# Key and query norms at the end of the projection's program, with another order of work in the sampled and mixing stages

## The chip, the cores and the metric

The kernel runs on one core of one Trainium2 chip. The metric is the device time of one execution in microseconds; three runs of a kernel are compared by their median.

## What is computed

One step of a one-layer hybrid decoder over 1104 tokens: 1040 of a prompt (16 meta tokens ahead) and 64 sampled ones, eight sequences of eight. Cut to what the change touches:

```
proj = rmsnorm(x) @ w_in                       # 1024 -> 5136 columns, split into three head groups
q, k = l2norm(silu(conv(q))) * 128**-0.5, l2norm(silu(conv(k)))
beta = sigmoid(b); g = -exp(a_log) * softplus(a + bias); G = cumsum(g) in a chunk
# gated DeltaNet, per chunk and head: A = I + tril(beta k k') exp(G_i - G_j); solve with [beta v, beta k exp(G)]
o = (q exp(G)) S + tril(q k' dec) w;   S = exp(G_last) S + (k exp(G_last - G))' w
# Mamba-2 SSD, per chunk: y = tril(C B' dec) xdt + (C exp(G)) h;  h = exp(G_last) h + B' xdt
# short convolution of 512 channels; then
x = x + concat(gated norms of the three) @ w_out;  x = x + moe(rmsnorm(x));  y = rmsnorm(x)
```

The prompt goes through in chunks from a zero state. The sampled tokens start from given states, so that each of their eight sequences has its own 128x128 state per head.

## The kernel before

Activations are held transposed, channels on partitions and tokens along the free axis. All products of the projections are made of three products of split operands (`copy_hi` on ScalarE takes a rounded high part, `take_lo` on VectorE the rest). The stages are separate programs, one `Block` each with one instruction list per engine, and a stage starts when every engine has ended the one before. Inside a stage the order is written out by hand; semaphores named in `REC_PE`, `SAM_DVE` and the like count steps, and SP and POOL issue the DMAs in the order written, waiting in line.

**Projection** (`projection_phase`). 40 blocks of 128 columns, two PSUM halves. VectorE scales, convolves and splits weights, ScalarE applies silu. The last 12 blocks are the short convolution; VectorE's last step there (L604 to L614) ends in a store by POOL (L435), a second one for the kept rows (L476), and SP waits for both (L336). `Gates` makes the gate rows early in the stage: `rows_a`, `rows_b`, `rows_c` hold four or twelve rows each at partitions 0, 32, 64, 96.

**Recurrence** (`recurrence_phase`). Before the first chunk it squares keys and queries (L904), sums them over the channels with a picking matrix on TensorE (L1114), takes logarithms on ScalarE (L907, L910) and puts them into the rows on VectorE (L995 to L1004), so that the l2 norms are folded into the decay exponents. SP stores three of the row groups to `g_dram` (L801 to L803) and, when these have landed, loads rows of it broadcast over the partitions, for each chunk: `rc_gb` (L783, L778), `rc_eb` (L791), `rc_egs` (L793). Ahead of that SP loads `x`, `bcs`, `d_skip` and the first `rc_gb` half (L796 to L798, L778). TensorE turns the rows into columns (L1123). POOL makes the decay tables (L826 to L843) and decayed states (L852, L854); then ten chunks of 104 tokens follow, one chain through the engines each.

**Sampled tokens** (`sampled_phase`). SP loads the rows table `ds_gb`, the two states `ds_s` and `ds_ss` and `d_skip`, in this order. ScalarE's exponential of the table comes first, VectorE multiplies it onto the keys, TensorE multiplies the 64 small pieces of the keys with the eight states (L1501), then the triangular products, then the queries with the states (L1501), the SSD pieces (L1546), and the state updates (L1560, L1571) with operands spread over the sequences by VectorE. `S1` and `spread` have two buffers for four heads.

**Output projection** (`mix_phase`). Nine tiles of 128 tokens. `w_out` comes in eight chunks of 768 KB through two landing buffers (`chunk`), each split by ScalarE and VectorE. VectorE's `gate` makes the gated rows; `scale` normalises them; TensorE's `out(t, h)` makes half h of tile t, 36 products. `gate` waits for four constants:

```
dve.wait_ge(consts, 64)
dve.scalar_tensor_tensor(mix[:, 0:4, 0:n], q[:, :, cols(t)], ow[:, 0:1], z[:, 0:4, 0:n], ...)
```

After it `expert_phase` sorts the tokens by expert and runs 33 blocks of experts; it isn't touched.

Of the kernel before, what the change touches and what calls it, by code (L numbers as in the profile page):

```python
# [17 lines left out]
ALU = mybir.AluOpType  # L18
# [3 lines left out]
P = 128  # L22
# [236 lines left out]
def projection_phase(nc, io, hn, gates, q, kv, ones, masks, xbc_dram, z_dram, yc_dram):  # L259
# [6 lines left out]
    with ExitStack() as stack:  # L266
# [6 lines left out]
        w1, rb = m.sb("c_w1", [P, KD]), m.sb("c_rb", [P, T])  # L273
        qkv, x, sq, ss_of = (q, kv[:, 0:HA], kv[:, HA:2 * HA]), kv, out, 1
# [7 lines left out]

        def pair(name):
            return [m.sem(f"c_{name}{h}") for h in range(2)]
# [4 lines left out]
        x_hi, x_lo = m.sem("c_xhi"), m.sem("c_xlo")  # L289
# [22 lines left out]
        with nc.Block() as block:  # L312
# [26 lines left out]
            def _(pe):  # L339
# [25 lines left out]
                with pe.Fori(1, NB_ALL // 2) as i:  # L365
                    for h in range(2):
                        pe.wait_ge(lo_done[h], i + 1)
                        pe.wait_ge(ps_free[h], i + 1)
                        block_(i, h)

            @block.scalar
            def _(act):
# [49 lines left out]
                for b in range(3 * NC - 2):  # L422
                    split_hi(act, *divmod(FIRST_C + b, 2))

# [54 lines left out]
            def _(dve):  # L479
# [66 lines left out]
                dve.wait_ge(gates.dve_step, 16)  # L546
                convolve(3, 1)
# [19 lines left out]
                for b in range(3 * NC):  # L567
# [10 lines left out]
                    if b < 3 * NC - 2:  # L578
                        split_lo(dve, i, h)
                    if b % 3 == 1:  # L580
# [17 lines left out]
                    if b % 3 == 2:  # L598
# [15 lines left out]
                        dve.tensor_tensor(o, o, rb[:], ALU.mult).then_inc(yc_done, 1)  # L614

# [55 lines left out]
def recurrence_phase(nc, io, qkv, x, bcs, rows, columns, g_dram, masks, xbc_dram):  # L671
# [16 lines left out]
    with ExitStack() as stack:  # L688
# [8 lines left out]
        dve_set, squared, summed, logs, rows_done, rows_sent = (m.sem("rc_set"), m.sem("rc_sq"), m.sem("rc_sum"),  # L697
                                                                m.sem("rc_log"), m.sem("rc_rows"), m.sem("rc_sent"))
# [6 lines left out]
        NQK, CB = 2 * HA, 4  # L705
        sq, pick, eps = sb("sq", [P, 2, T]), sb("pick", [P, NQK, 36]), sb("eps", [64, 1])
        spare = sb("spare", [64, 3])
        lnk, lnq = sq[:, 0], sq[:, 1]
# [20 lines left out]
        sums = ps[:, 5:8, 0:TW]  # L729
# [9 lines left out]

        def by_tile(ap):  # L740
            return ap.rearrange("p (n t) -> p n t", n=NT)
# [31 lines left out]
        def _(sp):  # L773
# [29 lines left out]
            sp.dma_start(g_dram[R_Q:R_K], lnq[ROW_G:ROW_G + HA, :]).then_inc(rows_sent, 16)  # L803
# [13 lines left out]
        def _(pool):  # L817
# [27 lines left out]
            pool.wait_ge(dve_set, 14)  # L845
# [13 lines left out]
            pool.wait_ge(dve_set, 5)  # L859
# [7 lines left out]
        def _(act):  # L867
# [33 lines left out]
            for b in range(NQK):  # L901
                if b >= 2:
                    act.wait_ge(summed, b - 1)
                act.activation(sq[:, b % 2, :], (keys, queries)[b // HA][:, b % HA, :], ACT.Square).then_inc(squared, 1)  # L904
            act.wait_ge(dve_set, 14)
            act.wait_ge(summed, NQK)
            act.activation(by_tile(lnq[ROW_G:ROW_G + HA, :]), sums[ROW_G:ROW_G + HA], ACT.Ln,  # L907
                           bias=eps[ROW_G:ROW_G + HA]).then_inc(logs, 1)
            act.wait_ge(rows_done, 1)
            act.activation(lnk[ROW_G:ROW_G + HA, :], lnk[0:HA, :], ACT.Ln).then_inc(logs, 1)  # L910
# [54 lines left out]
        def _(dve):  # L965
# [5 lines left out]
            dve.memset(pick[:], 0.0).then_inc(dve_set, 1)  # L971
            dve.memset(eps[:], DK * EPS).then_inc(dve_set, 1)
            dve.wait_ge(dve_set, 1)
            for b in range(NQK):
                at = b if b < HA else ROW_G + b - HA
                ins = dve.memset(pick[:, b, at:at + 1], 1.0 if b < HA else float(DK))
            ins.then_inc(dve_set, 1)
# [6 lines left out]
            dve.wait_ge(dve_set, 9)  # L984
            dve.tensor_tensor(neg16_t[:], neg16[:], neg_t, ALU.add).then_inc(dve_set, 1)
            dve.tensor_tensor(neg_off[:], neg_off[:], neg, ALU.add).then_inc(dve_set, 1)
            dve.wait_ge(dve_set, 11)
            dve.tensor_tensor(neg16[:], neg16[:], neg, ALU.add).then_inc(dve_set, 1)
            dve.scalar_tensor_tensor(neg16_t[:], ident, NEG, neg16_t[:], ALU.mult, ALU.add).then_inc(dve_set, 1)
            dve.wait_ge(dve_set, 13)  # L990
            dve.sem_inc(dve_set, 1)

# [1587 lines left out]
```

## Time and profile before

| what | value |
|---|---|
| median of 3 runs | 1576.05 us (1573.89 to 1579.41) |
| profiled execution | 1573.76 us, its span 1572.1 us |
| busy: TensorE | 1396.8 us (89%) |
| busy: VectorE, ScalarE, POOL | 947.4 (60%), 624.2 (40%), 308.8 (20%) |
| mean granted TensorE clock | 0.918 of full |
| recurrence starts | 541.94 |
| sampled stage starts | 830.85 |
| output projection starts | 936.56 |

Times are microseconds from the first instruction. A busy share is a mean over stages with different limits; what an edit is worth has to be read in its own stage. PE is TensorE's products, PEld its weight loads, DVE VectorE, ACT ScalarE, POOL GpSimd, SPq the queue of SyncE that issues most DMAs.

### The profile page before, as it was taken

Reading aid. Unit: us, or ns where it says so; the run is one execution under the profiler, and the core shown is the slowest. Engines: PE = TensorE matmul, PEld = TensorE weight load, DVE = VectorE, ACT = ScalarE, POOL = GpSimd, SP = SyncE. Lnnn points to the kernel's source line nnn. Section 1 sums busy time; section 2 is a strip of 40 time slices with the busy share of each in tenths; the row PEclk is TensorE's granted clock in tenths of the full one; section 3 lists DMA queues with packets and bytes.
Section 4 is the critical chain, followed back from the end, with each engine's and each line's share of the span. In section 5 each row is a group of like instructions: output and inputs, shape, how many; then the busy total and the mean of one; then the engine's idle time right before and its main releaser. Section 6 shows DMA issues by size and latency. Waiting matters only on the chain. (4 is left out here: it accounts for less than half of the span.)

```text
span 1572.1 us, 22657 instructions
## 1 busy us (share of the span) xinstructions
PE 1396.8 (89%) x8385; PEld 1246.3 (79%) x8385; DVE 947.4 (60%) x1307; ACT 624.2 (40%) x917; POOL 308.8 (20%) x328
## 2 busy tenths in 40 slices
PE   7899999999999769999997944999984999999990
PEld 5899999999999549998996813888863788888870
DVE  4579666421334227777662446555428899999973
ACT  5231212121001154454541004332322888888874
POOL 0011111100000026546430000100001333333321
PEclk9999999999999879999995556999985999999995
DMA  5011122223111253543513036523315699899948
GB/s 203 27 41 40 40 82 83 105 83 105 60 54 42 81 128 66 100 97 70 111 34 141 1 155 194 169 81 119 95 50 205 215 278 276 266 277 275 269 78 270
DMA packets 113207, 199.12 MB, mean 127 GB/s; under 512 B 63292, under 2 KB 84028, under 8 KB 108004
## 3 DMA queue, kind: packets, MB, share of 16 engines
q1 hardware_dynamic: 97556, 140.70, 28.6%
q0 software_dynamic: 15568, 57.37, 13.3%
q8 instruction: 46, 0.75, 0.2%
q14 instruction: 37, 0.30, 0.1%
HBM read 202.12 MB, written 49.41 MB: 160 GB/s over the span
## 5 line engine op out<-in xcount | busy, mean ns | idle before, releaser
L98 PE MATMUL c_ps<-hn_lo,c_whi 128*128 128x368 f32 x936 | 177.9, 332 | 5.6 <-DVEq L182 5.6
L98 PE MATMUL c_ps<-hn_hi,c_wlo 128*128 128x368 f32 x936 | 177.5, 332 | 0.0
L98 PE MATMUL c_ps<-hn_hi,c_whi 128*128 128x368 f32 x936 | 176.6, 331 | 0.0
L98 PEld LDWEIGHTS c_ps<-hn_lo,c_whi 128*128 128x128 f32 x936 | 160.8, 189 | 5.8 <-issue 5.8
L2233 DVE TENSOR_TENSOR e_winlo<-e_win,e_winhi 128x2048 fp32r<-128x2048 f32 x66 | 151.2, 2292 | 20.9 <-ACT e_winhi L2161 18.8
L98 PEld LDWEIGHTS c_ps<-hn_hi,c_wlo 128*128 128x128 f32 x936 | 160.8, 189 | 0.0
L98 PEld LDWEIGHTS c_ps<-hn_hi,c_whi 128*128 128x128 f32 x936 | 159.8, 188 | 0.0
L82 ACT CAST c_whi<-c_w 128x1024 fp32r<-128x1024 f32 x40 | 42.1, 1052 | 227.5 <-PE c_ps L98 227.5
L2161 ACT CAST e_winhi<-e_win 128x2048 fp32r (+1 forms) x66 | 122.7, 1914 | 5.5 <-DMA e_win<-in_w_gate_up 4.6
L2074 POOL DMA_INDIRECT x_rows<-e_ys,idx_out x33 | 81.8, 2478 | 146.7 <-ACT e_ys L2186 146.7
L526 DVE SCALAR_TENSOR_TENSOR c_y<-c_raw,c_taps,c_y 128x1128 f32<-128x1128 f32 x60 | 83.6, 1394 | 6.1 <-DVE c_y L522 0.2
L2408 DVE TENSOR_TENSOR e_wdnlo<-e_wdn,e_wdnhi 128x2048 fp32r<-128x2048 f32 x33 | 75.5, 2289 | 4.0 <-ACT e_wdnhi L2171 3.5
L87 DVE TENSOR_TENSOR c_wlo<-c_w,c_whi 128x1024 fp32r<-128x1024 f32 x40 | 48.7, 1217 | 47.4 <-ACT c_whi L82 47.4
L2171 ACT CAST e_wdnhi<-e_wdn 128x2048 fp32r (+1 forms) x33 | 63.2, 1916 | 32.6 <-PE e_psd L2125 21.4
L485 DVE TENSOR_TENSOR c_raw<-c_ps,c_rb 128x368 f32<-128x368 f32 (+1 forms) x80 | 30.0, 437 | 64.4 <-PE c_ps L98 63.7
L2101 PE MATMUL e_psg<-e_winhi,e_hthi 128*128 128x512 f32 x264 | 66.4, 394 | 0.0
L2101 PE MATMUL e_psg<-e_winlo,e_hthi 128*128 128x512 f32 x264 | 65.3, 390 | 0.0
L2101 PE MATMUL e_psg<-e_winhi,e_htlo 128*128 128x512 f32 x264 | 65.3, 389 | 0.0
L871 ACT COPY rc_m<-rc_ps 104x208 f32<-104x208 f32 x120 | 39.7, 332 | 64.2 <-PE rc_ps L1099 63.8
L1677 POOL DMA_DIRECT2D x_rows<-o_land x9 | 4.9, 540 | 303.7 <-ACT o_land L1725 303.7
L1873 PE MATMUL o_psx<-o_whi,o_mixhi 128*128 128x512 f32 (+1 forms) x216 | 57.7, 419 | 3.8 <-ACT o_mixhi L82 3.8
L2101 PEld LDWEIGHTS e_psg<-e_winhi,e_hthi 128*128 128x128 f32 x264 | 50.1, 191 | 10.6 <-ACT e_hthi L2178 0.2
(477 smaller groups left out, 2792.1 us busy)
## 6 DMA issues: line engine op xcount, KB each, us to landing
e_win<-in_w_gate_up SPq DMA_DIRECT2D x33, 2048.0 KB
e_wdn<-in_w_down SPq DMA_DIRECT2D x33, 1024.0 KB
c_w<-in_w_in SPq DMA_DIRECT2D x40, 512.0 KB, 3.3
rc_eb<-g_rows SPq DMA_DIRECT2D x10, 1040.0 KB, 5.9
o_land<-in_w_out SPq DMA_DIRECT2D x8, 768.0 KB, 5.5
x_rows<-o_land POOLq DMA_DIRECT2D x12, 512.0 KB, 4.5
rc_gb<-g_rows SPq DMA_DIRECT2D x10, 507.0 KB
kv<-in_xT SPq DMA_DIRECT2D x4, 1104.0 KB, 9.7
```

Of the source, the lines that this page charges most:

```text
L82: return eng.copy(dst, src)
L87: return dve.tensor_tensor(dst, src, hi.bitcast(F32), ALU.subtract)
L98: mm = pe.matmul(dst, left(x, k), right(z, k), start=(n == 0 and k == 0), stop=(n == 2 and k == ks - 1))
L526: op = dve.scalar_tensor_tensor(y[:, h, 0:CONVW], raw[:, h, j:j + CONVW], tap[:, j:j + 1], y[:, h, 0:CONVW], ALU.mult, ALU.add)
L871: act.copy(dst, src).then_inc(a.sem, 1)
L1873: mm = pe.matmul(ps_x[0:n, t % 2, h, :], mixed[a][:, t % 2, k, 0:n], w_r[b][:, 4 * h:4 * h + 4, k, :], start=False, stop=(i == 2 and k == ...
L2074: pool.indirect_dma_start(x2_dram, bass.IndirectOffsetOnAxis(ap=idx_out[:, o:o + 1], axis=0), ys[:, o % YB, :], None, compute_op=ALU.add). ...
L2101: mm = pe.matmul(ps_g[:, r % 2, :], ht[a][:, r % 2, k, :], win_r[b][:, r % 2, k, :], start=(i == 0 and k == 0), stop=(i == 2 and k == KD - 1))
L2161: act.copy(win_r[0][:, r % 2, ks, :], landed(win, here)[:, ks, :]).then_inc(win_hi, 1)
L2171: act.copy(wdn_r[0][:, r % 2], landed(wdn, here)).then_inc(wdn_hi, 1)
L2233: dve.tensor_tensor(win_r[1][:, r % 2, ks, :], landed(win, here)[:, ks, :], win_r[0][:, r % 2, ks, :].bitcast(F32), ALU.subtract).then_inc ...
L2408: dve.tensor_tensor(wdn_r[1][:, r % 2], landed(wdn, here), wdn_r[0][:, r % 2].bitcast(F32), ALU.subtract).then_inc(wdn_lo, 1)
```

## The change

It does four things. (1) The squares of keys and queries, their sums and the logarithms leave the recurrence and become the end of the projection's program. They use the projection's PSUM half 0 and two spare buffers (`y` and the landing buffer of the weights). The logarithms are written into rows of `rows_b`; copies of the gate rows that VectorE needs beside them are put into `rows_c` early in the projection. In the recurrence four VectorE steps are left. (2) The table of the sampled rows, now `ahead.gb`, is loaded during chunk 3 of the recurrence. (3) The sampled stage has another order: triangular and b, x, cb products ahead of the products with the states; `S1` is gone and the state is decayed in place, after the queries have read it; `spread` has four buffers; the second SSD spread, the last products, additions and the store go by halves; `ds_ss` is asked for when `ds_s` has landed. (4) In the output projection `w_out` has three landing buffers, the two small constants are loaded right after the first gate tile, and the other two count on the semaphore of `xt`, for which the first residual product and the first norm wait; semaphore pairs are merged.

```diff
@@ projection_phase
+        squares, product = (y[:, 1, 0:T], late[:, 0:T]), y[0:HA, 0, 0:T]
+        sums = ps[:, 0, :, 0:TW]
...
             (TensorE, after the last block)
+                pe.wait_ge(ps_free[0], NB_ALL // 2 + 1)
+                pe.wait_ge(picked, 2)
+                for b in range(NQK):
+                    pe.wait_ge(squared, KD + b + 1)
+                    for n in range(NT):
+                        mm = pe.matmul(sums[0:36, n, :], pick[:, b, :], squares[b % 2][:, n * TW:(n + 1) * TW],
+                                       start=(b == 0), stop=(b == NQK - 1))
+                    mm.then_inc(summed, 1)
             (ScalarE, after its last cast)
+                for b in range(NQK):
+                    if b >= 2:
+                        act.wait_ge(summed, KD + b - 1)
+                    act.activation(squares[b % 2], (qkv[1], q)[b // HA][:, b % HA, :], ACT.Square).then_inc(squared, 1)
+                act.activation(spare, eps, ACT.Ln)
+                act.wait_ge(summed, KD + NQK)
+                act.wait_ge(mean, 5)
+                act.activation(by_tile(rows[1][q3, :]), sums[rg], ACT.Ln, bias=eps[rg])
+                act.activation(rows[1][q2, :], product, ACT.Ln)
+                act.activation(rows[1][q0, :], product, ACT.Ln)
             (VectorE, early, and at its end)
+                dve.tensor_copy(rows[2][q0, :], rows[1][rg, :])
+                dve.tensor_copy(rows[2][q2, :], rows[0][rg, :])
+                dve.tensor_copy(rows[2][q3, :], rows[0][rg, :])
...
+                dve.wait_ge(summed, KD + NQK)
+                dve.scalar_tensor_tensor(by_tile(product), sums[0:HA], EPS, by_tile(rows[0][0:HA, :]), ALU.add,
+                                         ALU.mult).then_inc(mean, 1)
@@ recurrence_phase (the squares, sums, logarithms and their five VectorE steps are removed)
             (SP)
-            sp.wait_ge(rows_done, 6)
+            sp.wait_ge(rows_done, 5)
...
+                if c == 3:
+                    sp.dma_start(ahead.gb[:], g_dram[:, TP:T].partition_broadcast(P)).then_inc(ahead.gb_loaded, 16)
             (VectorE, first)
+            dve.scalar_tensor_tensor(rows_a[q3, :], rows_b[q2, :], -0.5, rows_c[q2, :], ALU.mult, ALU.add).then_inc(rows_done, 1)
...
+            dve.scalar_tensor_tensor(rows_b[q1, :], rows_b[q0, :], -0.5, rows_c[q0, :], ALU.mult, ALU.add).then_inc(rows_done, 1)
@@ sampled_phase
             (SP)
-            sp.dma_start(gb[:], g_dram[:, TP:T].partition_broadcast(P)).then_inc(gb_loaded, 16)
             sp.dma_start(S[:], io["state_gdn"]).then_inc(state_moved, 16)
+            sp.wait_ge(state_moved, 16)
             sp.dma_start(SS[:], io["state_ssd"]).then_inc(sstate_moved, 16)
...
+            for half in range(2):
+                wait(v, f"ss1_{half}")
+                sp.dma_start(io["new_ssd_s"][:, seqs], SS[:, seqs]).then_inc(sstate_moved, 16)
             (VectorE)
+            wait(p, "o_state")
+            for h in range(HA):
+                tt_(S[:, :, h, :], S[:, :, h, :], last_of(h).to_broadcast([P, NSEQ, DK]), ALU.mult)
...
+            for half in range(2):
+                wait(p, f"sds0_{half}")
+                spread_xdd(1, 4 * half, 4)
             (TensorE: this stands now behind the mt, bt, xt and cb products)
             pe.wait_ge(state_moved, 16)
             wait(v, "kg")
             with_states(tall(0), kg)
@@ mix_phase
+    LAND = 3
             (SP)
             load_z(0)
-            chunk(0)
-            load_yc(0)
-            chunk(1)
-            load_xt(0)
             sp.dma_start(ow[:], io["onorm_a"]).then_inc(consts, 16)
             sp.dma_start(yw[:], io["onorm_b"]).then_inc(consts, 16)
-            sp.dma_start(w2r[:], io["norm2_row"].partition_broadcast(P)).then_inc(consts, 16)
-            sp.dma_start(wr[:], io["w_router"]).then_inc(consts, 16)
-            for n in range(2, KD):
+            chunk(0)
+            chunk(1)
+            load_yc(0)
+            chunk(2)
+            load_xt(0)
+            sp.dma_start(w2r[:], io["norm2_row"].partition_broadcast(P)).then_inc(xt_loaded, 16)
+            sp.dma_start(wr[:], io["w_router"]).then_inc(xt_loaded, 16)
+            for n in range(LAND, KD):
                 chunk(n)
             (VectorE, gate)
-                dve.wait_ge(consts, 64)
+                dve.wait_ge(consts, 32)
             (TensorE, carry)
-                pe.wait_ge(xt_loaded, 16 * (t + 1))
+                pe.wait_ge(xt_loaded, 16 * (t + 3))
```

## Rows read from the trace of the kernel before

**Rows 1.** Windows: start:end length, PE, PEld, DVE, ACT, POOL (count), clock, DMA share, GB/s.

```profile
532.11:541.94 9.83, 0.00 (x0) 0.00 (x0) 2.74 (x4) 0.00 (x0) 1.07 (x2) 0.70 0.15 61
541.94:559.76 17.82, 16.55 (x48) 5.73 (x48) 2.59 (x20) 8.88 (x8) 0.00 (x0) 0.88 0.78 274
552.00:556.00 4.00, 4.00 (x15) 1.46 (x13) 0.00 (x0) 2.25 (x2) 0.00 (x0) 1.00 0.99 338
```

**Rows 2.** Timeline, recurrence head: start, length, engine, line, operation, [idle before, releaser].

```profile
541.94 0.42 SPq L796 DMA_DIRECT2D x<-xbc_rows  x1
...
559.80 1.30 DVE L995 SCALAR_TENSOR_TENSOR rc_sq<-rc_ps,rows_a 4x1104 f32<-4x1104 f32 x1 [14.87 <-PE rc_ps L1114]
...
561.14 1.17 ACT L907 ACTIVATE rc_sq<-rc_ps,rc_eps 4x1104 f32<-4x1104 f32 x1
...
568.38 0.29 SPq L803 DMA_DIRECT2D g_rows<-rc_sq  x1
...
570.42 0.31 SPq L783 DMA_DIRECT2D rc_gb<-g_rows  x1
...
575.33 0.88 POOL L826 TENSOR_TENSOR rc_dect<-rc_gb,col_a 104x416 f32<-104x416 f32 x1 [2.64 <-DMA rc_gb<-g_rows]
...
583.24 0.38 DVE L1027 SCALAR_TENSOR_TENSOR rc_m<-rc_ps,rc_dec 104x208 f32<-104x208 f32 x1 [6.09 <-ACT rc_dec L878]
```

**Rows 3.** DMA issues, 541.9 to 560: operation, KB each, us from issue to landing.

```profile
bcs<-xbc_rows SPq DMA_DIRECT2D x1, 2208.0 KB, 14.6
...
rc_skip<-in_d_skip SPq DMA_DIRECT2D x1, 2.0 KB, 14.3
```

**Rows 4.** Timeline of SP and POOL, chunk 3 of the recurrence.

```profile
653.28 0.57 SPq L783 DMA_DIRECT2D rc_gb<-g_rows  x1
...
660.54 0.88 POOL L826 TENSOR_TENSOR rc_dect<-rc_gb,col_a 104x416 f32<-104x416 f32 x1 [10.61 <-DVE rc_qkt L969]
```

**Rows 5.** Busy time by stretch, chunk 3.

```profile
655.00:661.00 6.00, 5.97 (x62) 5.72 (x62) 4.67 (x14) 4.70 (x15) 0.46 (x1) 1.00 1.07 177
```

**Rows 6.** DMA issues of the sampled stage.

```profile
new_ssd_s<-ds_ss SPq DMA_DIRECT2D x1, 2048.0 KB, 6.2
...
ds_gb<-g_rows SPq DMA_DIRECT2D x1, 768.0 KB, 6.0
```

**Rows 7.** Busy time by stretch, sampled stage.

```profile
830.85:841.79 10.94, 4.01 (x25) 3.10 (x25) 4.05 (x10) 1.70 (x3) 1.32 (x4) 0.50 0.90 310
...
855.54:862.72 7.18, 6.89 (x48) 5.48 (x47) 2.62 (x5) 1.47 (x4) 0.00 (x0) 0.50 0.00 0
...
876.47:880.78 4.31, 3.08 (x18) 2.52 (x17) 3.09 (x8) 0.37 (x1) 0.00 (x0) 0.50 0.00 0
...
908.27:920.14 11.87, 7.03 (x9) 2.33 (x8) 10.30 (x8) 0.00 (x0) 0.00 (x0) 0.50 0.42 177
...
927.37:936.56 9.19, 0.00 (x0) 0.00 (x0) 2.48 (x4) 0.00 (x0) 0.00 (x0) 0.50 0.54 228
```

**Rows 8.** Groups of instructions, sampled stage: count | busy us, mean ns | idle before.

```profile
L1501 PE MATMUL ds_ps<-ds_qg,ds_s 128*128 128x8 f32 x64 | 13.8, 361 | 0.0
...
L1546 PE MATMUL ds_ps<-ds_cs,ds_ss 128*64 128x8 f32 x128 | 11.0, 255 | 0.7 <-DVE ds_cs L1416 0.7
...
L1359 DVE TENSOR_TENSOR ds_ss<-ds_ss,ds_eb 128x4096 f32<-128x4096 f32 x1 | 4.4, 4414 | 0.0
```

**Rows 9.** Timeline, head of the output projection.

```profile
942.47 1.47 ACT L82 CAST o_whi<-o_land 128x1536 fp32r<-128x1536 f32 x1 [50.29 <-DMA o_land<-in_w_out]
...
948.69 0.75 DVE L1774 SCALAR_TENSOR_TENSOR o_mix<-q,o_ow,o_z 128x512 f32<-128x512 f32 x1 [7.42 <-DMA o_wr<-in_w_router]
...
961.64 5.13 PE L1873 MATMUL o_psx<-o_whi,o_mixhi 128*128 128x512 f32 x12 [3.84 <-ACT o_mixhi L82]
...
983.42 4.63 PE L1873 MATMUL o_psx<-o_whi,o_mixhi 128*128 128x512 f32 x12
...
995.05 2.98 PE L1873 MATMUL o_psx<-o_whi,o_mixhi 128*128 128x512 f32 x12
```

More of the change, by code:

```diff
@@ L273, in projection_phase @@
         w1, rb = m.sb("c_w1", [P, KD]), m.sb("c_rb", [P, T])
+        NQK, rg = 2 * HA, slice(ROW_G, ROW_G + HA)
+        late = w[:].rearrange("p a k c -> p (a k c)")
+        pick = late[:, T:T + NQK * 36].rearrange("p (b c) -> p b c", b=NQK)
+        eps, spare = (late[0:64, T + NQK * 36 + i:T + NQK * 36 + i + 1] for i in range(2))
+        squares, product = (y[:, 1, 0:T], late[:, 0:T]), y[0:HA, 0, 0:T]
+        q0, q2, q3 = (slice(a, a + HA) for a in (0, 64, 96))
         qkv, x, sq, ss_of = (q, kv[:, 0:HA], kv[:, HA:2 * HA]), kv, out, 1
@@ L668, with recurrence_phase @@
 REC_POOL = ["q", "t", "qm", "tm", "d", "doff", "d16", "s", "sm"]
[L671 removed]
+def recurrence_phase(nc, io, qkv, x, bcs, rows, columns, ahead, g_dram, masks, xbc_dram):
     L, HP, HPG = CH, HA // 2, HB // GB
@@ L899, in scaled @@
                 ins.then_inc(a.sem, 1)
[L901 to L910, printed above, removed]
+            act.wait_ge(dve_set, 12)
             for c in range(NCH + 1):
@@ L1108, in prod @@
                 products(view(bank[b]), lhs, rhs_, range(g * HP, (g + 1) * HP)).then_inc(p.sem, 1)
-            pe.wait_ge(dve_set, 3)
-            for b in range(NQK):
-                pe.wait_ge(squared, b + 1)
-                for n in range(NT):
-                    mm = pe.matmul(sums[0:36, n, :], pick[:, b, :], sq[:, b % 2, n * TW:(n + 1) * TW], start=(b == 0),
-                                   stop=(b == NQK - 1))
-                mm.then_inc(summed, 1)
-            pe.wait_ge(rows_done, 6)
+            pe.wait_ge(rows_done, 5)
             for c in range(NCH + 1):
@@ L1346, in _ @@
             copy(bt[:], bank[6][0:L, 0:GB * NB].rearrange("p (g s) -> p g s", g=GB))
+            wait(p, "ks_state")
+            copy(kst2[:], tall(0))
             wait(p, "m4")
@@ L1436, in _ @@
             wait(v, "w")
-            spread_w(0)
-            spread_w(1)
-            spread_xdd(0)
+            for h in range(HA):
+                tt_(spread[:, h], w[:, h, :].unsqueeze(1).to_broadcast([TS, NSEQ, DK]),
+                    seq_of.to_broadcast([TS, NSEQ, DK]), ALU.mult)
+            spread_xdd(0, 0, NSEQ)
+            dve.wait_ge(sstate_moved, 16)
+            wait(p, "sy_state")
+            last = eb[:, R_SSD:R_Q, :].rearrange("p h (b t) -> p b h t", t=LSEQ)[:, :, :, LSEQ - 1:LSEQ]
+            tt_(SS[:], SS[:], last.to_broadcast([P, NSEQ, HB, PB]), ALU.mult)
             wait(a, "o_state")
@@ L1515, in _ @@
             prod(sq_(5), M, mt)
-            wait(a, "ks_state")
-            turn(wide(7), kst2, full)
             wait(q, "x_st")
```

277 lines of the change are left out of this document (131 added, 146 removed).

## The prediction

> **What bounds the kernel now.** I read the shares of busy time first (TensorE 89% of the span), then the waits, then the timeline over the three joins that the change touches, and last the DMA view. The projection, the output projection from its second tile on and the experts keep TensorE full, and no edit shortens those. At the joins one chain runs alone and its waits are the time.
>
> Join 1, projection to recurrence: TensorE stands still for 9.83 us while the last short convolution is written out; then 48 matmul passes sum squares (16.55) [rows 1]. Five 1.30 us steps and two logarithms of 4-row tiles follow, three row writes go out by 568.4, the broadcast rows land at 575.33, POOL builds tables for 7.9 us, and VectorE starts chunk 0 at 583.24, which is 41.3 after the recurrence's start at 541.94 [rows 2].
>
> Join 2, the sampled stage, 830.85 to 936.56: TensorE is granted 0.50 of its clock throughout, the lower of its two levels (1.2 GHz), and is nearly always busy or waited for [rows 7]. Its holes are the first 10.94 us (4.01 busy), 4.84 us in the stretch at 908.27 where it waits for one spread tile, and 9.19 us of tail.
>
> Join 3, the head of the output projection: TensorE starts its first product 25.1 us after the stage starts, the second half of tile 0 at 46.9 and tile 1 at 58.5 [rows 9].
>
> **Squares and logarithms in the projection's end.** Nothing is removed: 8 squares, 24 matmuls and the logarithms move ahead. TensorE is at its upper clock level when it ends at 532.11, so a pass takes 0.31 (13 weight loads in 4.00 us [rows 1]); 48 make 14.85, to 547.2. ScalarE's squares fit under that: 8 at 1.1 (8.88 busy [rows 1]) against 1.85 for the six passes of each. Its table switch for the logarithm is put behind the last square, under the last passes. Then, in series, the product 1.30 and now three logarithms of 1.17 [rows 2], as the first waits for the product: 4.8 with hand-offs, to 552.0. With 0.5 for the join the recurrence starts at 552.5, 10.6 later. The convolution's tail (9.83) is covered by the squares; run ahead of them it would add its whole length. The pick memsets and the three 4-row copies on VectorE (about 0.7 each) fall where it waits for TensorE.
>
> The recurrence then needs four steps of 1.3, to +5.5, where before it needed 25.8. Taken alone that gives 20.3 back, and 9.7 net. But the three row writes stand on SP's queue behind x, bcs, d_skip and the first table load, which are still issued at +0 to +2. The 2 KB d_skip, issued half a microsecond after bcs, took 14.3 us against bcs's 14.6 [rows 3]: a small transfer does not overtake, and it landed at 557.25, +15.3, with the 338 KB of the table load still behind it. Before, the writes went into an empty queue; now they wait. I let them land at +17.5 (queue empty at about +16, then 1.5 to 2, as from 568.4 to 570.42 [rows 2]). From there 4.9 to the broadcast and 7.9 to chunk 0 as before: +30.3 against +41.3. So 11.0 comes back and 10.6 is paid: **-0.4**. Bounds: -9.7 if the writes don't wait, +1.5 if landing takes 2 us more.
>
> Beside it: the Trainium skill, page "DMA: Bandwidth & Descriptors", section "Queues, rings and completion order", says that on each DMA engine descriptors are taken in ring order, and also that completion is not first-in first-out per issuing engine, since a copy may use fewer rings. By the first half this edit is worth nothing, by the second it could give the 9.7; the d_skip row agrees with the first, and no run here shows a row write behind a long load.
>
> **The sampled rows' table loaded ahead.** 768 KB in 256-byte pieces (landing 6.0 us alone [rows 6]) move from the sampled stage into chunk 3, onto SP's queue between that chunk's table rows and the next chunk's gate rows. DMA is full there: from 655 to 661 its share is 1.07 [rows 5]. The gate rows were issued at 653.28 and POOL took them at 660.54, when VectorE let it [rows 4]; about 2 us of that was slack, and 3.5 to 4 us of transfer now goes before. POOL's tables come some 2.8 late, and behind them on POOL stand the state decays, which VectorE and through it TensorE wait for at the chunk's end. I take **+2.0**, once; bounds 0 and +4.
>
> **The sampled stage.** TensorE stays the bound, so I follow it.
> - Start to the key-state products: 10.94 before, set by table, exponential, and the 2 MB state queued behind the table. Now the tables are there; VectorE's ten small instructions of this stretch (4.05 busy [rows 7]) start at once, and two products with the decay follow, at +5.6. The state alone lands about as 2 MB do elsewhere, 6.2 [rows 6], so near +7. TensorE does its squarings and the b, x and cb products, moved here, until +9.4. Then 13.75 of state products, and only 2.6 instead of 7.18 of small ones before the query-state products (13.8 [rows 8]). These start at +25.8 instead of +31.9: 6.1.
> - Between them and the SSD-state products: 4.31 [rows 7] becomes 3.4, as the operand is ready: 0.9.
> - Four spread tiles instead of two, and decay in place: VectorE does these under the 11.0 us of SSD-state products, and the 4.4 us decay of the SSD state [rows 8] now stands ahead of its output additions, on which the release of the first heads' banks waits. TensorE then waits for the first added state only at its third head, with 2 us to spare. 0.
> - The second SSD spread goes by halves as the first products retire: 11.87 becomes 7.03, the busy time of that stretch [rows 7]: 4.8.
> - Tail 9.19 [rows 7]: half the last additions (1.25 saved) and half the last store, 1 MB instead of 2 (2.3 of 6.2 saved): 3.6.
>
> Sum **-15.4**. Bounds -18 and -9: the low end is a first stretch that ends with the state at +7, the high end one where the added-state margin is missed and the store's half costs nearly the whole.
>
> **The head of the output projection.** VectorE's second gate waited until 948.69, +12.1, for router weights that it doesn't read [rows 9]; with the small constants ahead of the weights it runs at +4.7. Weight 0 still lands at about +6 (ScalarE took it at +5.9 [rows 9]), so its low part is done at +9.4 instead of +14.5. With three landing buffers chunk 2 is already on its way and chunk 3 is asked for at +9.4 instead of +16. ScalarE, VectorE and the mean's reciprocals then run through to the first mixed tile, ready at +20.2 (before +25.0): products at +20.3. Weight 7 is asked for at +25.7 and split by +33.3; tile 1's gate, sums and the second half of tile 0 follow at +35.7, against +46.9: 11.2. From there to tile 1 the 11.6 us of products are the same [rows 9]. I take **-11.1**. Bounds -13 (TensorE's hole ahead of tile 0's second half shrinks so far that the half-clock group there, 4.63 us at 983.42 against 2.98 later [rows 9], also runs fast) and -5 (only the first product's 4.8). Carry 0 now waits for the broadcast norm row too; it lands near +14.4 where carry 0 starts, at no cost while the first products wait for the mix.
>
> **Sum.** -0.4 + 2.0 - 15.4 - 11.1 = -24.9 on the profiled execution's 1573.76 (span 1572.1 and 1.7 around it): 1548.9. The median of the three runs, 1576.05, is 2.3 above that execution; I give half of it: 1550.
>
> **Rivals.**
> 1. The row writes don't wait for x and bcs. For: they touch four partitions only. Against: d_skip's 14.3 us. Then chunk 0 starts 9.7 earlier instead of 0.4, and 1550 becomes 1540.7. Chance 0.14.
> 2. The weights keep the head of the output projection. Splitting a chunk is 1.5 on ScalarE and 1.75 on VectorE, eight times, and the last ones still wait for their transfer as before. For: ScalarE's first cast, at 942.47, was released by its transfer [rows 9], and so are later ones. Against: three buffers ask for them 7 us earlier. Then only 4.8 of 11.1 comes: 1556. With the sampled stage at its poor end: 1562. Chance 0.15.
> 3. Slower: the clock of TensorE in the output projection. The place is tiles 1 to 8. A group of 12 products took 5.13 at 961.64 and 2.98 at 995.05 [rows 9]; a tile has six groups, so a tile at half clock costs 12.9 more, and from two tiles on the 25 is gone: with three, 1550 + 39 = 1589. For: the stage already fell to half clock in its own gap. Against: from tile 1 on TensorE has no gap to fall in. Chance 0.03.
> 4. The change doesn't do what it says: the sampled stage's order hides nothing, as another wait ends at the same time, and join 1 costs its +1.5: 1573 or so. Chance 0.03.
>
> **How the numbers follow.** Forecast 0.65, by itself 1544 to 1557. The range 1539 to 1561 takes in the first rival and most of the second. A difference under 0.3% (4.7 us) can't be told from none here. Faster 0.94, the same 0.02, slower 0.04.
>
> **What would show it.** Right: in the new trace the 48 passes start at about 532.4 at 0.31 each; the recurrence starts near 552.5; the row writes are issued near 558 and not awaited before 569; chunk 0 starts within 2 us of 583. TensorE's state products follow the cb products, its second SSD products follow the first with no hole, and the sampled stage lasts about 90 us instead of 105.7; tile 1's products start about 47 after the stage's start. Wrong: a recurrence that starts chunk 0 before 578, a sampled stage above 97, or a gap of the old size ahead of tile 0's second half.

## The result and the profile after

The changed kernel took 1552.06 us (median of 4 executions, 1547.32 to 1555.68), beside 1575.55 for the kernel before in the same job (1573.89 to 1579.41): over all executions a ratio of 0.9846, 95% interval 0.9813 to 0.9878. The forecast was 1550.0, with a range of 1539 to 1561. A second job with the same kernel (below) gave 1555.15 against 1574.71, 0.9878 (0.9862 to 0.9895). By the two ratios the change is worth 24 and 19 us. The profiled execution has a span of 1550.1 against 1572.1, 22.0 less.

The page of the profile after: span, and busy time of the engines with their shares and instructions.

```profile
span 1550.1 us, 22656 instructions
...
PE 1396.8 (90%) x8385; PEld 1247.9 (81%) x8385; DVE 955.2 (62%) x1312; ACT 624.4 (40%) x919; POOL 308.6 (20%) x328
```

Where the 22.0 us come from, read off the starts of the same instructions in both traces:

| stretch | before | after | difference | forecast |
|---|---|---|---|---|
| start to chunk 0's first product on VectorE | 583.24 | 582.93 | -0.31 | -0.4 |
| chunk 0 to the sampled stage | 247.61 | 248.67 | +1.06 | +2.0 |
| sampled stage | 105.71 | 89.65 | -16.06 | -15.4 |
| output projection, start to tile 1 | 58.49 | 48.15 | -10.34 | -11.1 |
| tile 1 to the end | 577.05 | 580.70 | +3.65 | 0 |

**Join 1.** Timeline of the changed kernel, from the projection's end to chunk 0: start, length, engine, line, operation, idle time before it and what ended it.

```profile
531.86 1.51 PE L98 MATMUL c_ps<-hn_hi,c_whi 128*128 128x368 f32 x8
533.30 2.05 PE L386 MATMUL c_ps<-c_y,c_w 128*36 128x368 f32 x6
...
546.34 2.02 PE L386 MATMUL c_ps<-c_w 128*36 128x368 f32 x6
...
552.10 1.12 ACT L456 ACTIVATE rows_b<-c_y 4x1104 f32<-4x1104 f32 x1
553.48 0.42 SPq L839 DMA_DIRECT2D x<-xbc_rows  x1
...
558.90 5.47 SPq L844 DMA_DIRECT2D g_rows<-rows_a  x1
...
568.77 1.68 PE L1122 MATMUL rc_ps<-kv 128*104 128x104 f32 x8 [3.39 <-DMA bcs<-xbc_rows]
...
569.88 0.31 SPq L826 DMA_DIRECT2D rc_gb<-g_rows  x1
570.10 1.57 POOL L886 TENSOR_TENSOR rc_dect<-rc_gb,col_a 104x832 f32<-104x832 f32 x1 [29.30 <-DMA rc_gb<-g_rows]
...
575.03 0.88 POOL L871 TENSOR_TENSOR rc_dect<-rc_gb,col_a 104x416 f32<-104x416 f32 x1 [1.34 <-DMA rc_gb<-g_rows]
...
582.93 0.38 DVE L1050 SCALAR_TENSOR_TENSOR rc_m<-rc_ps,rc_dec 104x208 f32<-104x208 f32 x1 [16.07 <-ACT rc_dec L923]
```

The squares' passes run from 533.30 to 548.36 (15.06 for 48), the last logarithm ends at 553.2, and the recurrence starts 11.5 later than before [rows 2]. Its first row write is issued at +5.4. That issue alone lasts 5.47, where a row write took 0.29 before [rows 2], and the three writes have landed only at 569.88, +16.4. What was saved ahead of the row writes is waited for in their queue. POOL's SSD tables stand in the same line: their rows, issued behind bcs, came at 570.10; chunk 0 doesn't wait for that, as POOL then idles another 1.34 us for the gate rows at 575.03.

**The sampled stage.** TensorE's products of the changed kernel, from the key-state products on.

```profile
840.58 13.82 PE L1521 MATMUL ds_ps<-ds_kg,ds_s 128*128 128x8 f32 x64
...
857.08 13.66 PE L1521 MATMUL ds_ps<-ds_qg,ds_s 128*128 128x8 f32 x64
...
874.25 11.02 PE L1566 MATMUL ds_ps<-ds_cs,ds_ss 128*64 128x8 f32 x128
...
888.01 13.96 PE L1580 MATMUL ds_ps<-ds_spread,ds_kd 64*128 64x512 f32 x16
901.77 13.86 PE L1592 MATMUL ds_ps<-ds_sspread,ds_bt 64*128 64x512 f32 x16
```

State products start at +8.98 (before +10.94 with the small ones still to come), query-state products at +25.48, and the two sets of SSD products (901.77) are one run without the hole that the stretch at 908.27 had [rows 7]; 5.62 are left from the last product to the end, against 9.19 [rows 7]. By the starts of the same groups 6.4 us are won up to the query-state products, 0.9 up to the SSD-state products, 5.2 in the SSD products and 3.6 in the tail.

**The output projection's head.** First groups of products: tile 0 first half, second half, tile 1.

```profile
942.02 5.49 PE L1896 MATMUL o_psx<-o_whi,o_mixhi 128*128 128x512 f32 x12 [2.03 <-ACT o_mixhi L82]
...
957.71 4.69 PE L1896 MATMUL o_psx<-o_whi,o_mixhi 128*128 128x512 f32 x12
...
969.40 2.98 PE L1896 MATMUL o_psx<-o_whi,o_mixhi 128*128 128x512 f32 x12
```

They stand at +20.77, +36.46 and +48.15 after the stage's start; before they stood at +25.1, +46.9 and +58.5 [rows 9].

**The last stretch.** The 3.65 us lie behind the output projection's products. Busy time by stretch around the last expert block, first of the kernel before, then of the changed one (behind the five engines stand PE's granted clock, the DMA share and GB/s).

```profile
1530.00:1540.00 10.00, 5.23 (x21) 3.38 (x19) 2.34 (x2) 5.93 (x7) 3.93 (x2) 0.98 0.44 75
```

```profile
1505.00:1515.00 10.00, 7.18 (x23) 4.75 (x21) 2.72 (x2) 4.22 (x6) 2.41 (x1) 0.83 0.44 87
```

In the changed kernel's execution the clock fell among the last products (0.83 against 0.98), and its last four pairs of products took 4.26 us instead of 2.58; from the last pair on it is 36.1 to the end instead of 35.0, and ahead of the experts 0.7 were lost. No edit touches this stretch, and in the other executions of this case the time from the last pair on was anything from 33.4 to 37.1. But not all of it is chance. Tile 1 to the end took 577.2 to 581.6, on average 579.2, in the eleven executions that have the new stages, and 577.05 and 576.80 in the two with the old ones. From the last product of the output projection to the experts' first on a gathered tile (`e_pst`) it was 45.0 to 45.9 in those eleven, and 44.7 and 44.6 in those two. So about 2 us seem to come with the change; why stays open.

### The profile page after: what moved, and what is told of

It is laid out like the page before. It is cut to its first block and busy times, and to the rows that moved or that the text cites. A ratio compares the mean times of both kernels' runs of the same rounds, so it can differ in the third digit from the quotient of the medians.

```text
span 1550.1 us, 22656 instructions
## 1 busy us (share of the span) xinstructions
PE 1396.8 (90%) x8385; PEld 1247.9 (81%) x8385; DVE 955.2 (62%) x1312; ACT 624.4 (40%) x919; POOL 308.6 (20%) x328
## 5 line engine op out<-in xcount | busy, mean ns | idle before, releaser
L1804 DVE RECIPROCAL o_sq<-o_sq 128x512 f32<-128x512 f32 (+1 forms) x9 | 29.0, 3219 | 48.5 <-ACT o_sq L1728 48.3
```

## The experiments

All carry the changed kernel's edits unless it says otherwise. Marks of their profiled executions, in us; the ratio is to the kernel before, with its interval. "Head" is from the recurrence's start to chunk 0's first product, "chunk 3" the interval between the broadcast loads of chunks 3 and 4, "to tile 1" counts from the output projection's start. The changed kernel's ratios in its two jobs differ by 0.0032, which is 5 us, so small steps are judged by the marks of the stretch that an edit touches.

| kernel | ratio | head | chunk 3 | sampled stage | to tile 1 |
|---|---|---|---|---|---|
| before | 1 | 41.30 | 23.93 | 105.71 | 58.49 |
| changed | 0.9846 (0.9813 to 0.9878) | 29.45 | 26.70 | 89.65 | 48.15 |
| changed, second job | 0.9878 (0.9862 to 0.9895) | 30.09 | 27.44 | 90.37 | 48.71 |
| squares only | 0.999 (0.9981 to 0.9999) | 29.76 | 23.94 | 105.72 | 60.20 |
| rows ahead of bcs | 0.9859 (0.9844 to 0.9874) | 29.75 | 26.67 | 89.66 | 51.29 |
| rows on ScalarE's queue | 0.9846 (0.9832 to 0.9859) | 28.45 | 26.75 | 90.37 | 50.23 |
| rows ahead, waits later | 0.9827 (0.9801 to 0.9854) | 24.10 | 27.95 | 85.92 | 49.91 |
| table in the last chunk | 0.9827 (0.9813 to 0.984) | 30.04 | 23.83 | 85.61 | 50.27 |
| table in the sampled stage | 0.9887 (0.9866 to 0.9909) | 29.15 | 24.04 | 95.85 | 48.78 |
| spread not by halves | 0.9879 (0.9858 to 0.99) | 29.16 | 28.40 | 91.85 | 50.20 |
| two landing buffers | 0.99 (0.988 to 0.9919) | 29.79 | 28.39 | 89.33 | 54.90 |
| rows ahead, waits later, table last | 0.981 (0.9797 to 0.9824) | 24.40 | 23.95 | 90.36 | 47.85 |
| the same, x and bcs split | 0.9799 (0.9785 to 0.9812) | 21.87 | 24.03 | 89.16 | 48.48 |

**Squares only.** The kernel before with the first part of the change alone.

```diff
 # sampled_phase and mix_phase as before; no early table
+# projection_phase and recurrence_phase as changed
```

> The kernel before with the squares, sums and logarithms at the projection's end as the only edit; the sampled stage and the output projection are as before. Theory (the row writes queue behind x and bcs on SP's queue, so what the recurrence's head saves is given back): the recurrence starts about 11.5 us later than before (553.5 against 541.94), chunk 0 within 1 us of before (582 to 584), time -0.4 +- 1.5 us, a ratio of 0.999 to 1.001. Rival (the row writes do not wait, and the wait seen in the changed kernel's trace has another cause there): chunk 0 near 573.5, -9.7 us, ratio 0.994.

Measured: 1575.36 us, ratio 0.999, which is -1.6 us with an interval of -3.0 to -0.2. The head in that kernel's timeline:

```profile
552.70 0.42 SPq L839 DMA_DIRECT2D x<-xbc_rows  x1
...
558.12 5.75 SPq L844 DMA_DIRECT2D g_rows<-rows_a  x1
...
582.46 0.38 DVE L1048 SCALAR_TENSOR_TENSOR rc_m<-rc_ps,rc_dec 104x208 f32<-104x208 f32 x1 [15.02 <-ACT rc_dec L921]
```

The recurrence starts at 552.70 and chunk 0 at 582.46, against 583.24 [rows 2]. The theory holds, the rival is out: by itself the edit moves 11 us of work forward and gets at most 3 us back.

**Rows ahead of bcs.**

```diff
 x; load_gs(0)
-bcs; d_skip
 wait rows_done; three row writes; wait rows_sent
 load_gg(0); load_eb(0)
+bcs; d_skip
```

> The changed kernel, with only the order of SP's queue at the recurrence's start altered: x and the first table rows, then the three row writes, the gate rows and the broadcast rows for chunk 0, and bcs and d_skip after these. Theory (one queue is served in its order, and the bcs load held the row writes up): the row writes are issued at +5.4 into a queue that has only x and the table rows in it, land near +10, the broadcast rows near +15, POOL's tables end near +23 and chunk 0 starts there instead of at +29.45, while bcs lands near +19: -6.5 us (-4 to -8), 1545.5. Rival (the wait is not for bcs: the row writes need their 11 us wherever they stand, or the time comes back as bcs lands late): within 2 us of the changed kernel, 1552.

Measured: 1553.36 us, no gain, as the rival had it, and yet the theory's first half is right. The gate rows, bcs, POOL's last table of chunk 0 and TensorE's first key products in that kernel's timeline:

```profile
564.27 0.31 SPq L826 DMA_DIRECT2D rc_gb<-g_rows  x1
...
570.42 0.61 SPq L848 DMA_DIRECT2D bcs<-xbc_rows  x1
...
575.00 1.06 POOL L880 TENSOR_TENSOR rc_dec<-rc_dec,rc_neg 104x416 f32<-104x416 f32 x1
...
580.82 1.68 PE L1122 MATMUL rc_ps<-kv 128*104 128x104 f32 x8 [16.04 <-DMA bcs<-xbc_rows]
```

The row writes have landed at 564.27 instead of 569.88 and POOL is done at 576.06 instead of 581.8. But bcs is now issued at 570.42 instead of 553.95. TensorE idles 16.04 us for it, as it waits for bcs ahead of chunk 0 though the key products don't read it, and chunk 0 starts at +29.75. In the changed kernel that wait ended at 568.77 and cost nothing, since POOL's tables kept chunk 0 until 582.93 (Join 1, above). So the edit made a new wait of the old one's length: that the two are so nearly equal is chance.

**Rows on ScalarE's queue.**

```diff
+act: wait rows_done; three row writes
 act: column copies
+act: wait rows_sent; load_gg(0); load_eb(0)
 sp:  load_gs(0); x; bcs; d_skip
-sp:  row writes; load_gg(0); load_eb(0)
```

> The changed kernel, with the row writes, the gate rows and the broadcast rows of chunk 0 issued on ScalarE's queue, the first table rows ahead of x on SP's, and x and bcs behind them on SP's as before. Theory that queues share the DMA engines in turn: the row writes land near +8 though x and bcs are under way, the broadcast rows near +14 as they share the bandwidth, chunk 0 starts near +22: -7 us (-4 to -9). Rival (the engines work off what was issued first, whatever queue it came by): the row writes land near +16 as in the changed kernel, 0 +- 2 us.

Measured: 1552.44 us; the head is 1.0 shorter (28.45). On its own queue a row write is issued in 0.25 to 0.53 us while x and bcs are under way on SP's, so it was the queue that held its issue. The landing is another matter: the gate rows follow 6.9 us after the first row write, where 2.7 were enough in the kernel before (567.73 to 570.42), so the writes don't land near +8 as the theory had it, nor near +16 as the rival had it. ScalarE's column copies ahead of the gate rows end at the same time and may hide a part. The rows read back pay too:

```profile
552.37 0.33 SPq L821 DMA_DIRECT2D rc_gb<-g_rows  x1
...
557.80 0.53 ACTq L940 DMA_DIRECT2D g_rows<-rows_a  x1
...
564.74 0.32 ACTq L951 DMA_DIRECT2D rc_gb<-g_rows  x1
...
572.90 0.88 POOL L864 TENSOR_TENSOR rc_dect<-rc_gb,col_a 104x416 f32<-104x416 f32 x1 [8.46 <-DMA rc_gb<-g_rows]
```

From the gate rows' issue to POOL 8.2 us pass, where 4.9 did with nothing else under way [rows 2]; bcs lands 16.2 us after issue instead of 14.7. In time the rival's 0 is met, but not for its reason: transfers of both queues were under way together, and each took longer. The Trainium skill, page "DMA: Bandwidth & Descriptors", section "Queues, rings and completion order", says that an engine takes packets from its queue rows in turn; the 8.2 against 4.9 fit that, though no row here shows the turns.

**Rows ahead of bcs, and the waits for x and bcs at their first use.**

```diff
-pe, dve: wait x_loaded, b_loaded ahead of chunk 0
+pe:  chunk 0: wait x_loaded at the x transposes, b_loaded at the B transposes
+dve: chunk 0: wait x_loaded, const_loaded at the skip product
```

> The changed kernel, with the row writes, gate rows and broadcast rows of chunk 0 ahead of bcs on SP's queue, and TensorE's and VectorE's waits for x and bcs, which stood ahead of chunk 0, moved to the first use in it. Theory (with the new order alone, TensorE's wait for bcs took the place of the wait for the row writes; POOL's tables ended at 576.06, and bcs is used only 6.7 us into the chunk): TensorE's first key products run near 570, chunk 0's first table product on VectorE is at about 576.5 instead of 582.9, bcs lands near 580.7, before its first use at 583; -6 us against the changed kernel (-4.5 to -7), about 1546. Rival (the transfers' volume bounds the head: 4.4 MB of x and bcs have to come in some time, and chunk 1's rows queue behind them): chunk 0 starts 6 earlier and chunk 1 gets 4 or more of it back: -2 to 0 us.

Measured: 1548.22 us, ratio 0.9827: 3 us below the changed kernel by the ratio of its first job, 8 by that of its second. The first product on VectorE and POOL's tables of chunk 1:

```profile
577.96 0.38 DVE L1046 SCALAR_TENSOR_TENSOR rc_m<-rc_ps,rc_dec 104x208 f32<-104x208 f32 x1 [9.94 <-ACT rc_dec L923]
...
584.86 0.88 POOL L871 TENSOR_TENSOR rc_dect<-rc_gb,col_a 104x416 f32<-104x416 f32 x1 [7.92 <-DMA rc_gb<-g_rows]
```

The head is 24.10, 5.35 shorter, as the theory said. The rival has its part: POOL waits 7.92 us for chunk 1's rows, which are queued behind bcs (in the changed kernel it waited for VectorE there), and the intervals of chunks 0 to 2 are 0.7 longer each, so that some 2.2 go back. With another 1.25 in chunk 3, where the table's load falls, the stretch from the recurrence's start to the sampled stage is only 1.4 shorter in this execution, 276.7 against 278.1. By that mark it is the rival's range; the time leaves it open between the two.

**The table in the last chunk.**

```diff
-if c == 3:
+if c == NCH - 1:
     sp: ahead.gb <- g_dram[:, TP:T]
```

> The changed kernel, with the sampled rows' table loaded in the last chunk, where no chunk's rows stand behind it on SP's queue, instead of in chunk 3. Theory (in chunk 3 its transfer delays the next chunk's gate rows, and through POOL's tables the chunk): the interval from chunk 3's to chunk 4's broadcast load falls from 26.7 to about 24, the recurrence from chunk 0 on is about 1 us shorter (245.5 to 244.4), and the sampled stage is not later for it: -1 us (0 to -2). Rival (the chunk's delay has another cause, or the sampled stage then waits for the table): no shorter, or up to 3 us longer in the sampled stage's first 10 us.

Measured: 1549.28 us, with the same ratio as the version above. SP's queue in the changed kernel and in this one: the broadcast loads of chunks 3 and 4 and the table's load, and between them POOL's first gate table.

```profile
650.64 0.38 SPq L834 DMA_DIRECT2D rc_eb<-g_rows  x1
...
653.82 0.61 SPq L855 DMA_DIRECT2D ds_gb<-g_rows  x1
...
664.32 0.88 POOL L871 TENSOR_TENSOR rc_dect<-rc_gb,col_a 104x416 f32<-104x416 f32 x1 [13.75 <-DMA rc_gb<-g_rows]
...
677.34 0.38 SPq L834 DMA_DIRECT2D rc_eb<-g_rows  x1
```

```profile
649.87 0.38 SPq L834 DMA_DIRECT2D rc_eb<-g_rows  x1
...
660.30 0.88 POOL L871 TENSOR_TENSOR rc_dect<-rc_gb,col_a 104x416 f32<-104x416 f32 x1 [10.51 <-DVE rc_qkt L1005]
...
673.70 0.38 SPq L834 DMA_DIRECT2D rc_eb<-g_rows  x1
...
800.25 0.61 SPq L855 DMA_DIRECT2D ds_gb<-g_rows  x1
```

Chunk 3 takes 23.83 instead of 26.70, as the theory said. Behind the table's load POOL waits for the gate rows, 13.7 us from the broadcast load to its first table; without it POOL waits for VectorE, 10.4 us, and the rows are there. Over the case's executions with the load there it takes 26.67 to 28.40, and 23.83 to 24.04 without. The sampled stage is 4.0 shorter in this execution, and that is none of the edit's: its key-state products took 10.66 instead of 13.82, as they began with the clock up. Its first 20 us, and the first 10 of the changed kernel in its second job, where the clock never rose:

```profile
828.87:838.87 10.00, 8.19 (x67) 6.91 (x68) 9.76 (x22) 3.36 (x5) 1.72 (x4) 0.76 0.76 245
838.87:848.87 10.00, 10.00 (x61) 9.98 (x61) 0.53 (x2) 0.55 (x2) 0.00 (x0) 0.58 0.41 177
```

```profile
832.12:842.12 10.00, 8.27 (x52) 6.59 (x52) 8.69 (x19) 3.37 (x5) 1.72 (x4) 0.50 0.72 239
```

Of nine executions with this sampled stage two show the long rise (here and in the kernel with later waits, 85.61 and 85.92 us), four a shorter one that was over before the key-state products (89.16 to 89.66), and three none, with 0.50 throughout as in the kernel before (90.36 and 90.37); among these is the combined kernel, which has both edits. It is an accident of the execution worth up to 4.8 us, and a reason not to judge an edit by one profile's span.

**The table in the sampled stage again.**

```diff
-recurrence, chunk 3: sp: ahead.gb <- g_dram[:, TP:T]
+sampled stage, first on sp: ahead.gb <- g_dram[:, TP:T]
```

> The changed kernel, with the sampled rows' table loaded at the sampled stage's start, ahead of the state, as before, instead of in chunk 3 of the recurrence. Theory (the early table carries part of the sampled stage's gain and costs 2 us in the recurrence): the recurrence's 225.8 us from chunk 1's to the end's marks fall to 223.9; table, exponential and the state behind it let the state products start near +13 instead of +9.0: sampled stage 93 to 95 us instead of 89.7; together +2 us (0 to +4). Rival (the new order of the work alone hides the table): state products at +9 as now, -2 us.

Measured: 1557.58 us. Head of that sampled stage:

```profile
831.88 0.38 SPq L1329 DMA_DIRECT2D ds_gb<-g_rows  x1
...
838.17 0.42 DVE L1384 TENSOR_TENSOR ds_dec<-col_a,ds_gb 64x256 f32<-64x256 f32 x1 [5.80 <-DMA ds_gb<-g_rows]
...
847.04 13.18 PE L1520 MATMUL ds_ps<-ds_kg,ds_s 128*128 128x8 f32 x61
```

VectorE waits 5.80 us for the table, and the state products start at +15.16 instead of +8.98. The stage is 95.85: 6.2 of its 16.06 us hang on the early table. The recurrence did not get shorter in this execution (another chunk took 25.69, as one did before), and the time is 1.4 to 6.5 above the changed kernel's two jobs. The sign was right; the price of the missing table was 6.2 where I had expected 4.

**The second spread tile not by halves.**

```diff
-wait(p, f"sds0_{half}")
+wait(p, "sds0_1")
 spread_xdd(1, 4 * half, 4)
-pe: wait(v, f"sspread1_{half}")
+pe: wait(v, "sspread1_1")
```

> The changed kernel, with the second SSD spread tile written only when all first SSD products have retired, and TensorE's second products waiting for the whole of it. Theory (the halves took away the hole of 4.84 us that the stretch had before): a hole of 4.5 to 5 us between TensorE's first and second SSD products and the sampled stage 4.8 longer, +4.8 us. Rival (only the two spreads' own time, twice 1.22 and the hand-offs, was exposed, and the tail takes a part back): a hole of 2.5 to 3.5 us, and 2 to 3.5 us in time.

Measured: 1555.79 us, 5 above the changed kernel by the ratio of its first job and level with its second, so that the time decides nothing. TensorE's two sets of SSD products in that kernel:

```profile
902.02 7.03 PE L1592 MATMUL ds_ps<-ds_sspread,ds_bt 64*128 64x512 f32 x8
911.58 7.16 PE L1592 MATMUL ds_ps<-ds_sspread,ds_bt 64*128 64x512 f32 x8 [2.54 <-DVE ds_sspread L1385]
```

A hole of 2.54, and a stage 2.2 longer than the changed one: the rival. The two spread writes (2.35 together) are all that was exposed. In the kernel before the hole was 4.84 because VectorE did the state's additions (2.48) ahead of the second spread (2.27); the new order of VectorE's work gave that part, not the halves.

**Two landing buffers.**

```diff
-LAND = 3
+LAND = 2
 chunk(0); chunk(1); load_yc(0)
-chunk(2)
 load_xt(0); norm row; router weights
```

> The changed kernel, with two landing buffers for the output weights instead of three; the small constants stay ahead of the weights. Theory (as the prediction split it: the order of the constants brings the first product forward, the third buffer the rest): first product still at +20.8 after the stage's start, the second half of tile 0 at about +42 instead of +36.5 and tile 1 at +53.7 instead of +48.2: +5.5 us (+4 to +7). Rival (the constants' order did all of it): tile 1 within 1 us of +48.2, 0 +- 1 us.

Measured: 1559.98 us, 8.5 and 3.5 above the changed kernel by the ratios of its two jobs. Second half of tile 0 and tile 1 in that kernel (its stage starts at 923.48):

```profile
962.10 2.07 PE L1869 MATMUL o_psa<-o_sq,ones 128*128 128x512 f32 x2 [6.04 <-ACT o_sq L1719]
...
965.74 5.63 PE L1895 MATMUL o_psx<-o_whi,o_mixhi 128*128 128x512 f32 x12
...
978.38 2.98 PE L1895 MATMUL o_psx<-o_whi,o_mixhi 128*128 128x512 f32 x12
```

+42.26 and +54.90, as the theory expected: against the changed kernel's +48.15 the third buffer carries 6.8 us of the 10.34 and the constants' order 3.6. Tile 1 stood at +47.85 to +51.29, on average +49.4, in the ten executions with three buffers; by that average the split is 5.5 and 4.5. The constants' order by itself was not run. With two buffers TensorE idles 6.04 ahead of tile 1's sums, as ScalarE does them behind its last weight cast.

**The changed kernel again, and the combined ones.**

> The changed kernel once more, unaltered, beside the two versions below. Expected: 1552 us, ratio to the kernel before 0.9846 (0.982 to 0.988). Its profile is to show which terms vary between executions. Theory: the chunk behind the table's load takes 26.7 to 28.4 (without the load 23.9), the sampled stage 89.7 or, where TensorE keeps its upper clock through most of the key-state products, near 85.8; tile 1 of the output projection starts 48.2 to 51.3 after the stage's start. Rival (these numbers belong to the altered kernels, not to execution): 26.7, 89.65 and 48.15 again, each within 0.2.

> The changed kernel with both edits that made it faster: the row writes and chunk 0's rows ahead of bcs, with the waits for x and bcs at their first use, and the sampled rows' table loaded in the last chunk. Theory (the two act at different places and add up): chunk 0 at +24.1, every chunk near 24, -3 and -2.7 us: 1546.4 (1544 to 1549), ratio 0.981. Rival (both remove the same waiting for rows behind a full queue, so that the second adds nothing): 1549.

> As the version above, and of x and bcs only chunk 0's columns are loaded in the recurrence's head; the other columns follow behind chunk 1's rows. Theory (in the version with the new order alone some 2.3 of 5.35 us were given back in chunks 0 to 3, as chunk 1's rows queued behind bcs): chunk 0 starts at +22 to +23 instead of +24.1, chunks 1 and 2 are 24.0 again instead of 24.7; -2.5 us against the version above (-1 to -4), 1544. Rival (416-byte pieces and the rest's 3.9 MB ahead of chunk 1 cost as much as they save): 0 +- 1 us.

The last one's edit on top of the combined kernel:

```diff
-x, bcs <- all columns
+x, bcs <- columns of chunk 0
 ...
 chunk 1: load_gg(1); load_gs(1)
+x, bcs <- the other columns (waited for in chunk 1)
 load_eb(1)
```

Measured in one job: the changed kernel 1555.15, the combined one 1544.42, the split one 1541.89 (before 1574.71). In the changed kernel's new execution the chunk behind the table took 27.44, the sampled stage 90.37, and tile 1 stood at 48.71: the spread is the execution's. The two edits add up: the time falls by 10.7 us in this job, where 5.7 were expected, and by the marks of the two profiles the sampled stage starts 6.3 earlier (825.84 against 832.12). For the split the medians give another 2.5, which by themselves are within the intervals; its head is 2.5 shorter too (21.87 against 24.40), as the theory said. Head of the split kernel:

```profile
561.83 0.31 SPq L826 DMA_DIRECT2D rc_gb<-g_rows  x1
...
574.66 0.37 DVE L1049 SCALAR_TENSOR_TENSOR rc_m<-rc_ps,rc_dec 104x208 f32<-104x208 f32 x1 [8.51 <-ACT rc_dec L926]
```

```profile
x<-xbc_rows SPq DMA_DIRECT2D x1, 208.0 KB, 2.9
bcs<-xbc_rows SPq DMA_DIRECT2D x1, 208.0 KB, 4.9
```

Chunk 0's 208 KB of x land in 2.9 us instead of 8.1 for the whole, the row writes are through at +9.0, and chunk 0 starts at +21.87. Counted from the first instruction that is 8.6 us ahead of the kernel before (574.66 against 583.24); with the waits moved but x and bcs whole it was 5.3 and 4.8 (577.96 and 578.44). So only with the queue and the waits put in order does moving the squares ahead pay. What these edits would give without the moved squares was not run. The split kernel beats the changed one of the same job by 0.9% and the one before by 2.0%.

## Why the prediction was right, step by step

- **Squares and logarithms, -0.4: right**, -0.31 in the changed kernel and -0.78 alone. The mechanism is as told: row writes that wait behind x and bcs on one queue. That the number fits to 0.1 is in part luck, as two errors of 0.9 cancel: the recurrence started 11.5 later and not 10.6, and chunk 0 came at +29.45 and not +30.3, since the writes landed at +16.4 and not +17.5. One detail was missed: TensorE's wait for bcs stands ahead of chunk 0, so that putting bcs behind the rows gives nothing until that wait moves too. The 0.14 for rival 1 (the writes don't wait) went to something that 5.47 us of issue and 569.88 exclude.
- **Table ahead, +2.0: right in size**, though this pair of executions shows +1.06, as the kernel before had a chunk of 25.80 of its own. From chunk 1's broadcast load to the end of the recurrence the six kernels with the load in chunk 3 and the old place of the waits took 225.82 to 228.46, mean 226.9; four without took 223.64 to 225.62, mean 224.6: +2.3. The path is the forecast one, the gate rows late for POOL: its first table of chunk 4 starts 13.7 us after chunk 3's broadcast load, against 10.5 in the kernel before (650.01 to 660.54), so 3.2 later where 2.8 was forecast.
- **Sampled stage, -15.4: right**, -16.06. In the three executions whose clock stayed at 0.50 throughout, as the prediction took it, the stage took 90.36 or 90.37, which is -15.35; more came only in executions where the clock rose for a while. Its marks at +9.4, +25.8 came out at +8.98, +25.48, and its four terms of 6.1, 0.9, 4.8 and 3.6 at 6.4, 0.9, 5.2 and 3.6. One term was put down to the wrong cause: of the 4.8 us of the hole the halves give 2.2 to 2.5, the changed order of VectorE's additions the rest. The tail's halves have no run of their own. That the early table is the largest single piece, 6.2, was in the first two terms (10.94 to 9.4, and 7.18 to 2.6) but not said.
- **Head of the output projection, -11.1: right within an execution's spread**, -10.34 here; with the same code tile 1 stood at +47.85 to +51.29 in ten executions, and at +58.49 and +60.20 in two of the old one, on average -10.0. Rival 2 (the weights keep the head) is what two buffers show: there they keep 5 to 7 us of it.
- **The rest, 0: too low by about 2.** It is +3.65 in this execution, of which the clock and the tail's chance explain a part; the eleven executions with the new stages average 2.3 above the two with the old ones, for a reason that stays open. The projection is 1.26 longer ahead of the squares, which is part of the first row of the table; the recurrence's start lies at 552.37 to 554.04, on average 553.1, in the twelve runs with the same projection, against the forecast 552.5.

By averages over all executions that share a stretch, the five rows of the table are -0.5, +2.3, -16.8, -10.0 and +2.3, together about -23, between the two jobs' 19 and 24. The slower rival (half clock in tiles 1 to 8) did not come: tile 1's first group took 2.98, as before [rows 9].

## What to carry to other kernels

A step moved ahead is worth what its consumer's queue lets through: list every transfer that is issued ahead of its result on the same queue, and every wait that stands at a stage's start and not at the first use. When taking away a wait gives nothing, look for the wait that the edit itself made before the theory is dropped: here the load moved back was awaited too early, so that the order and the waits had to change together, and cutting the bulk loads to what the first chunk reads gave the rest. Put an early load where nothing urgent stands behind it on its queue, and judge by the stretch's own marks over several executions, since one profile's span moved by up to 4.8 us with the clock alone.

## What the runs showed of the hardware

- Issuing a 17 KB write behind 4.4 MB and the table rows on one queue kept SP for 5.47 us, against 0.29 in an empty one and 0.25 to 0.53 on ScalarE's queue at the same stage. The issue itself can be held, and with it everything behind it on that engine: in the kernel with the rows ahead, bcs was issued at 570.42 only, as the two 104 KB loads ahead of it took 5.00 to issue. It doesn't take x and bcs: in the kernel before, the same two loads took 4.92 with only chunk 0's gate and broadcast rows (507 and 1040 KB) ahead of them, and on ScalarE's queue they held ScalarE for 7.58. How much a queue takes before it holds the issue isn't shown.
- With the same instructions in the same order, TensorE's granted clock stayed at 0.50 through the sampled stage in three of nine executions; in four it rose to 1.00 and was back at 0.50 by 8 us into the stage, in two only by 11.6 us. What decides between them stays open. So does why one chunk near the middle of the recurrence takes 25.7 to 25.8 between broadcast loads in some executions without the table's load (before, the table in the sampled stage, the split kernel), and 23.9 in others.
